# Starting nine convolution accumulators on TensorE, and feeding the low weight halves from SBUF

## The reference, cut to what matters

```python
def conformer_conv_mixer(h, w_in, conv_w, conv_b, ln_g, ln_b, w_out):   # h: 512 x 1024
    proj = h @ w_in                                                     # 512 x 6144
    val, glu_gate, z = jnp.split(proj, 3, axis=-1)                      # 2048 channels each
    u = val * jax.nn.sigmoid(glu_gate)
    u = causal_depthwise_conv(u, conv_w) + conv_b                       # 31 taps per channel
    u = jax.nn.silu(layer_norm(u, ln_g, ln_b))
    return (u * jax.nn.silu(z)) @ w_out
```

## Time and profile before

| what | value |
|---|---|
| median of 3 runs | 2544.98 us (2544.66 to 2545.96) |
| the profiled execution, its own time | 2544.66 us |
| its span | 2542.9 us |
| TensorE busy | 2498.4 us (98%) |
| VectorE, ScalarE, GpSimd busy | 1459.5, 1289.4, 1519.5 us |
| mean granted TensorE clock | 0.997 of full speed |
| layer A, first time | about 22 to 304 us of the span |
| layer A, second time | about 1401 to 1682 us of the span |

### The profile page before, as it was taken

The page is one execution under the profiler, slowest core; times in us unless marked ns, Lnnn a source line. Parts: engine busy times, 40 slices in busy tenths (PEclk is TensorE's granted clock), DMA queues, the critical chain, the costliest instruction groups (busy, mean ns, idle before and its releaser), DMA issues.

```text
span 2542.9 us, 31601 instructions
## 1 busy us (share of the span) xinstructions
PE 2498.4 (98%) x11897; PEld 2029.2 (80%) x11897; DVE 1459.5 (57%) x2426; ACT 1289.4 (51%) x1994; POOL 1519.5 (60%) x1018
## 2 busy tenths in 40 slices
PE   8999999999999999999999999999999999999998
PEld 6888787878888787888888888878877678788887
DVE  6999863064565614444441899976598752523202
ACT  6889644266566533222232888854245553423322
POOL 5999665443453555444465799957435547545653
PEclk9999999999999999999999999999999999999999
DMA  7888622255556222222222778842322232222221
GB/s 209 191 183 183 149 102 99 102 145 147 133 145 147 93 99 84 99 100 97 91 97 98 180 178 186 183 118 95 123 104 67 88 127 97 100 98 88 96 99 67
DMA packets 72019, 310.75 MB, mean 122 GB/s; under 512 B 8043, under 2 KB 8267, under 8 KB 58300
## 3 DMA queue, kind: packets, MB, share of 16 engines
q1 hardware_dynamic: 49308, 225.11, 26.2%
q0 software_dynamic: 22560, 83.62, 16.8%
HBM read 302.81 MB, written 5.89 MB: 121 GB/s over the span
## 4 chain that ended last, share of the span: by engine, by line
PE 80%; DVE 10%; POOL 4%; issue 3%; ACT 3%; DMA 1%; DVEq 0%; SPq 0%; POOLq 0%; ACTq 0%
PE ps L64 78%; DVE ps L81 3%; POOL AR L73 3%; DVE AR L81 2%; PE ps L67 2%; DVE AR L73 1%; DVE HL L81 1%; ACT AR L70 1%; DMA WL<-in_weights 1%; POOL WL L115 1%; DVE X L73 1%; ACT L70 0%; DMA AR<-in_x 0%; ACT WL L70 0%; ACT HH L70 0%
## 5 line engine op out<-in xcount | busy, mean ns | idle before, releaser
L64 PE MATMUL ps<-HH,WH 128*128 128x512 f32 x3080 | 1213.2, 394 | 4.3 <-ACT HH L70 1.2
L64 PE MATMUL ps<-HL,WH 128*128 128x512 f32 x3080 | 1192.2, 390 | 1.3 <-DVE HL L81 1.3
L64 PE MATMUL ps<-HH,WL 128*128 128x512 f32 x3080 | 1095.9, 390 | 5.5 <-DMA WL<-in_weights 5.5
L73 POOL TENSOR_TENSOR WL<-WR,WH 128x1024 fp32r<-128x1024 f32 x278 | 694.5, 2521 | 648.0 <-ACT WH L70 647.9
L64 PEld LDWEIGHTS ps<-HH,WH 128*128 128x128 f32 x3080 | 578.5, 188 | 142.0 <-issue 9.7
L64 PEld LDWEIGHTS ps<-HH,WL 128*128 128x128 f32 x3080 | 579.0, 188 | 127.9 <-DMA WL<-in_weights 6.5
L64 PEld LDWEIGHTS ps<-HL,WH 128*128 128x128 f32 x3080 | 578.8, 188 | 120.6 <-DVE HL L81 2.6
L70 ACT ACTIVATE WH<-WR 128x1024 fp32r<-128x1024 f32 (+1 forms) x405 | 410.3, 1046 | 444.4 <-PE ps L64 444.3
L81 DVE SCALAR_TENSOR_TENSOR ps<-AR,VEC,ps 128x512 f32<-128x512 f32 x648 | 446.3, 751 | 7.1 <-ACT ps L70 1.6
L73 POOL TENSOR_TENSOR AR<-AR 128x512 f32<-128x512 f32 x210 | 323.3, 1807 | 10.7 <-DVE AR L73 1.9
L115 POOL DMA_DIRECT2D WL<-in_weights x127 | 149.5, 1177 | 178.5 <-ACT WL L70 178.5
(11 more groups left out here) (180 smaller groups left out, 2084.0 us busy)
## 6 DMA issues: line engine op xcount, KB each, us to landing
WR<-in_weights SPq DMA_DIRECT2D x106, 1024.0 KB, 4.8
WR<-in_weights SPq DMA_DIRECT2D x194, 512.0 KB, 4.8
WL<-in_weights POOLq DMA_DIRECT2D x127, 512.0 KB, 7.6
AR<-negc_rows POOLq DMA_DIRECT2D x16, 640.0 KB, 4.3
gate_rows<-WR SPq DMA_DIRECT2D x14, 256.0 KB, 2.0
AR<-gate_rows SPq DMA_DIRECT2D x14, 256.0 KB, 3.7
AR<-in_x SPq DMA_DIRECT2D x2, 1024.0 KB, 6.0
AR<-bias_by_distance POOLq DMA_DIRECT2D x1, 2048.0 KB, 8.5
```

What stands on the lines that cost most here:

```text
L64: return Op(None if self.e is None else self.e.matmul(o, l, r, start=first, stop=last, skip_group_check=True))
L73: return Op(None if self.e is None else self.e.tensor_tensor(o, a, b, op))
```

## The change

- Each of the last nine of the twelve chains is begun by TensorE, not by ScalarE. TensorE multiplies by two diagonal fp32 matrices (the taps 30 and 29 of the tile's channels), so that such a chain has 29 taps left for VectorE and not 30. ScalarE makes the diagonals out of the identity matrix, in a ring of five tiles in HT.
- POOL_TAPS and the allowances change: GpSimd now does four whole tiles and 24 taps of one more, from slot 3 on.
- The accumulating DMA reads the raw weights from the raw slot in SBUF, not from HBM; a raw slot is loaded again only after that DMA has landed.
- The second halves of the z chunks (eight in each layer A) are no longer made with a DMA: GpSimd subtracts.
- In slots 0 and 1 ScalarE and GpSimd do their splits in another order relative to begins and products.

```diff
-            return i == 0 and n == 1 or i in HEAD_CHUNK[1:] or any(f < i < f + KE + KE // 2 or i == f + KE + KE // 2 + 1 for f in FIRST_A)
+            return i == 0 and n == 1 or i in HEAD_CHUNK[1:] or any(f < i < f + KE + (KE // 2 if n == 0 else 0) or i == f + KE + KE // 2 + 1 for f in FIRST_A)
...
-                    if summed(before[-1], n):
-                        sp.wait_ge(w_hi, before[-1], n, "low")
-                    else:
-                        sp.wait_ge(w_lo, before[-1], n)
+                    wait_low(sp, before[-1], n)
...
-                            l = l.rearrange("p k c -> p (k c)")
-                        pool.dma_add(l, weights[i][:, n * 1024:(n + 1) * 1024]).then_inc(w_sum[i % 2][n], i, by=16)
+                            l, r = (t.rearrange("p k c -> p (k c)") for t in (l, r))
+                        pool.dma_add(l, r).then_inc(w_sum[i % 2][n], i, by=16)
...
+        DIAG = [HT[:, i * P:(i + 1) * P] for i in range(5)]
...
-        POOL_TAPS = {0: 8, 1: 10, 3: PAD, 7: PAD, 8: PAD, 12: PAD, 15: 18}
+        POOL_TAPS = {2: PAD, 4: PAD, 7: PAD, 10: PAD, 12: 24}
         CHAIN = [i for i in range(KE) if POOL_TAPS.get(i, 0) < PAD]
+        PE_BEGINS = CHAIN[3:]
+        LAST_TAP = {i: PAD - 2 if i in PE_BEGINS else PAD - 1 for i in CHAIN}
+        BY_PE = [(i, k) for i in PE_BEGINS for k in (PAD, PAD - 1)]
...
-                room = PAD * KE if rest else 14 + slot % 2 if slot < KE else 7 + (slot % 3 == 0)
+                room = PAD * KE if rest else (15) if slot < KE else (7)
...
-                room = PAD * KE if rest else 8 - (slot % 4 == 3) if slot < KE else 4 - (slot % 4 == 3)
+                room = PAD * KE if rest else (8) if slot < KE else (3 + slot % 2)
...
+                for i in PLAN[slot]["begin"]:
+                    if i in PE_BEGINS:
+                        pe.wait_ge(a_u, j, i)
+                        wait_chain_bank(pe, j, i)
+                        for k in (PAD, PAD - 1):
+                            pe.wait_ge(a_diag, j, i, k)
+                            pe.mm(chain_bank(i)[:, :], DIAG[BY_PE.index((i, k)) % 5], U[i][:, k:k + T], k == PAD,
+                                  k < PAD).then_inc(a_init_p, j, i, k)
...
+        def diagonals_scalar(act, j, i):
+            for k in (PAD, PAD - 1):
+                n = BY_PE.index((i, k))
+                if n >= 5:
+                    act.wait_ge(a_init_p, j, *BY_PE[n - 5])
+                act.act(DIAG[n % 5], ident[:, :], ACT.Copy, scale=conv_w(j, k, i)).then_inc(a_diag, j, i, k)
...
         def begins_scalar(act, j, at):
             for i in at["begin"]:
-                act.wait_ge(a_u, j, i)
-                wait_chain_bank(act, j, i)
-                act.act(chain_bank(i)[:, :], U[i][:, PAD:], ACT.Copy, scale=conv_w(j, PAD, i)).then_inc(a_init, j, i)
+                n = CHAIN.index(i)
+                if i not in PE_BEGINS:
+                    act.wait_ge(a_u, j, i)
+                    wait_chain_bank(act, j, i)
+                    act.act(chain_bank(i)[:, :], U[i][:, PAD:], ACT.Copy, scale=conv_w(j, PAD, i)).then_inc(a_init_a, j, i)
+                if n + 1 < len(CHAIN) and CHAIN[n + 1] in PE_BEGINS:
+                    diagonals_scalar(act, j, CHAIN[n + 1])
...
                 if slot < KE:
-                    if slot != 1:
-                        split_hi(act, c0 + slot + 1, (0, 1) if slot == 0 else (1,))
+                    split_hi(act, c0 + slot + 1, (0, 1) if slot == 0 else (1,))
...
-                    if slot == 0:
-                        begins_scalar(act, j, PLAN[slot])
                     split_hi(act, c0 + slot + 2, (0,))
-                    if slot > 1:
-                        begins_scalar(act, j, PLAN[slot])
+                    begins_scalar(act, j, PLAN[slot])
                     products_scalar(act, j, n[len(n) // 2:])
```

More of the change, by code:

```diff
@@ L828, in build_program @@
         a_sig, a_u, a_zs = sig("a_sig"), sig("a_u"), sig("a_zs")
-        a_init, a_tap, a_ev = (sig(n) for n in ("a_init", "a_tap", "a_ev"))
+        a_diag, a_init_p, a_init_a, a_tap, a_ev = (sig(n) for n in ("a_diag", "a_init_p", "a_init_a", "a_tap", "a_ev"))
         a_prod, a_add, a_turn, a_mom = sig("a_prod"), sig("a_add"), sig("a_turn"), sig("a_mom")
@@ L841, in build_program @@
         REST = DGS[1]
+        DIAG = [HT[:, i * P:(i + 1) * P] for i in range(5)]
         MV, MRS = ST[:, 384:392], ST[:, 392:396]
         BY = MV.rearrange("p (b s) -> p s b", s=2)
-        POOL_TAPS = {0: 8, 1: 10, 3: PAD, 7: PAD, 8: PAD, 12: PAD, 15: 18}
+        POOL_TAPS = {2: PAD, 4: PAD, 7: PAD, 10: PAD, 12: 24}
         CHAIN = [i for i in range(KE) if POOL_TAPS.get(i, 0) < PAD]
+        PE_BEGINS = CHAIN[3:]
+        LAST_TAP = {i: PAD - 2 if i in PE_BEGINS else PAD - 1 for i in CHAIN}
+        BY_PE = [(i, k) for i in PE_BEGINS for k in (PAD, PAD - 1)]
         POOLED = sorted(POOL_TAPS)
-        SHARED = [i for i in POOLED if POOL_TAPS[i] < PAD]
         Z_LATE = 3
         def conv_plan():
-            taps = {i: list(range(POOL_TAPS.get(i, 0), PAD)) for i in CHAIN}
+            taps = {i: list(range(POOL_TAPS.get(i, 0), LAST_TAP[i] + 1)) for i in CHAIN}
             adds = {i: list(range(PAD)) if POOL_TAPS[i] == PAD else list(range(1, POOL_TAPS[i])) + [PAD] for i in POOLED}
@@ L1084, in layer_a_vector @@
                     else:
-                        dve.wait_ge(a_init, j, i)
+                        if i in PE_BEGINS:
+                            dve.wait_ge(a_init_p, j, i, PAD - 1)
+                        else:
+                            dve.wait_ge(a_init_a, j, i)
                         dve.wait_ge(a_u, j, i)
@@ L1130, in layer_a_vector @@
             scaled_vector(dve, 3 * j, 3 * j + 1, vec["norm_mix_2" if j else "b_norm"])
+        def diagonals_scalar(act, j, i):
[4 more added lines that the diff above has]
+                act.act(DIAG[n % 5], ident[:, :], ACT.Copy, scale=conv_w(j, k, i)).then_inc(a_diag, j, i, k)
         def evacuate_scalar(act, j, i):
-            act.wait_ge(a_tap, j, i, PAD - 1)
-            if i in SHARED and i != SHARED[0]:
-                wait_conv(act, j, SHARED[SHARED.index(i) - 1])
-            o = REST if i in SHARED else U[i][:, PAD:]
+            act.wait_ge(a_tap, j, i, LAST_TAP[i])
+            o = REST if i in POOL_TAPS else U[i][:, PAD:]
             act.act(o, chain_bank(i)[:, :], ACT.Identity, bias=a_vec("a_conv_b", j, i)).then_inc(a_ev, j, i)
@@ L1182, in layer_a_scalar @@
                 if slot < KE:
-                    if slot != 1:
-                        split_hi(act, c0 + slot + 1, (0, 1) if slot == 0 else (1,))
+                    split_hi(act, c0 + slot + 1, (0, 1) if slot == 0 else (1,))
                     starts_scalar(act, j, PLAN[slot])
                     products_scalar(act, j, n[:len(n) // 2])
-                    if slot == 1:
-                        split_hi(act, c0 + slot + 1, (1,))
                     act.wait_ge(a_gate, j, slot)
@@ L1277, in layer_a_gpsimd @@
                 if slot < KE:
-                    if slot != 1:
-                        split_lo(pool, c0 + slot + 1, (0, 1) if slot == 0 else (1,))
+                    split_lo(pool, c0 + slot + 1, (0, 1) if slot == 0 else (1,))
                     if j == 0 and slot == 0:
@@ L1282, in layer_a_gpsimd @@
                     conv_gpsimd(pool, j, n[:len(n) // 2])
-                    if slot == 1:
-                        split_lo(pool, c0 + slot + 1, (1,))
                     split_lo(pool, c0 + slot + 2, (0,))
```

## The result

| | before | after |
|---|---|---|
| median | 2544.94 us (2544.66 to 2545.96) | 2570.27 us (2569.61 to 2573.34) |
| the profiled execution, its own time | 2544.66 us | 2571.78 us |
| its span | 2542.9 us | 2570.0 us |

The medians are those of four executions each. The changed kernel is slower by 25.3 us: the ratio is 1.010, 95% interval 1.0087 to 1.0112. 2571.0 was predicted.

What follows compares the result with a forecast made beforehand. TensorE, full in the slots, was taken as the bound. First layer +16.4 - 5 - 0.5 = +10.9, second +16.4 - 1.4 - 0.3 + 0.3 = +15.0, together +26 on 2544.66: 2571 us, range 2557 to 2586.

Steps and rivals of the forecast that it cites:

- main term: Layers A: 36 added fp32 matmuls on TensorE, nothing hiding them, cost 16.4 us a layer, 32.8 us in all.
- The price of a product: TensorE's begins: one fp32 matmul on 512 columns takes 0.91 us, four times a rounded one; bounds 0.455 and 0.99.
- The rival of half price: TensorE's begins: a diagonal product costs only its two records, 0.455 us each, giving 2554 us; chance 0.10.
- The start: TensorE's wait at 28 us and the clock fall go, about 6 us, of which 5 are kept; bounds 0 and 6.5.
- the reload: Raw slots in layers A, loaded only after the sum lands: just hidden with a 7.6 us landing, in layer B nothing.
- the late refill: Layers A: sums from SBUF take 12 us, ScalarE stands 3 us in each of 16 slots; 2590 to 2600; chance 0.12.
- The first tap and the single chains: First layer A: VectorE's first tap at 37 to 39 us, single chains 0.79 us a tap, slot 7's U at 122 to 125.
- The tails and the stall: Layers A: stall at 1618.69 goes, -1.4 us; GpSimd waits around last turns, net -0.5 us first, -0.3 second layer.
- Its lower end: Low end of the range, 2557 us: main sum with 0.82 us a matmul, full start gain and both tails free.
- What was costed at nothing: Layers A: ScalarE's changed work is worth nothing on the path; VectorE's taps stay inside TensorE's two-slot lead and cost nothing.
- GpSimd's part: Layers A: twelve adds fewer give -15 us, eight subtractions for DMA issues +11; GpSimd ends a few us less late.
- the price of VectorE without cover: VectorE's single chains in layer A: if the cover were gone, some 1 us a slot for four slots.

Runs made afterwards that it cites:

- the third product: Changed kernel with a third diagonal product before each TensorE begin, overwritten by the next, against the changed kernel: 2584.7 us, 1.0153 to before.
- the plan's row in the table: New plan and z subtraction only, all begins on ScalarE, sums from HBM, early reload, against the kernel before: 2561.0 us, 1.0058.
- one product a chain: Changed kernel without the tap 29 product in each TensorE begin, 18 of 36 left out, against the changed kernel: 2564.3 us, 1.0076 to before.
- all sums from SBUF alone: Kernel before with all 127 sums read from SBUF and raw slots reloaded only after their sum, against the kernel before: 2553.1 us, 1.0024.

## Why the prediction was right

**The time and its main term.** 2571.0 was predicted, 2570.3 measured. That TensorE is the bound, has no idle time to hide the products and pays for all 36 of them is shown three ways: by the chain (1.70 us a pair), by TensorE's begins alone, which make the kernel before as slow as the whole change does, and by the third product, which costs its full 0.86 us in the second layer.

**The price of a product** was mis-sized a little: 0.91 was taken, 0.85 measured. So the term is 18 x 0.85 = 15.3 us a layer and not 16.4, 2.2 us less in both. The distance in the earlier trace rows had the lead-in of the first matmul in it, as the text there says. A product is 3.7 times the 0.228 us of an ordinary matmul. The Trainium skill ("FP8 and Floating Point Precision", TensorE Precision Notes) gives true fp32 four passes; the measured 3.7 bears this out better than it does two. The two records of 592 ns of a product in the profile do not show it; the distance between its neighbours does. The rival of half price has fallen with it.

**The start** gave at its own place what was forecast: the first sum landed after 5.42 us, at 27.7, TensorE had no wait and its clock stayed at 1.00. At the first turn it was 90.92 - 85.50 = 5.4 us ahead of before. The forecast kept 5 us for good; 5.4 - 3.26 - 1.7 = 0.4 were left behind the wait at 93 us. The step that failed is the reload. It was forecast just hidden, ScalarE without a wait over 1 us. In the timeline of ScalarE in the changed kernel stand (the last line is in the second layer):

```profile
36.83 1.06 ACT L70 ACTIVATE WH<-WR 128x1024 fp32r<-128x1024 f32 x1 [9.18 <-DMA WR<-in_weights]
...
69.98 1.06 ACT L70 ACTIVATE WH<-WR 128x1024 fp32r<-128x1024 f32 x1 [3.64 <-DMA WR<-in_weights]
...
128.91 1.06 ACT L70 ACTIVATE WH<-WR 128x1024 fp32r<-128x1024 f32 x1 [3.35 <-DMA WR<-in_weights]
...
161.89 1.06 ACT L70 ACTIVATE WH<-WR 128x1024 fp32r<-128x1024 f32 x1 [2.04 <-DMA WR<-in_weights]
...
1442.39 1.06 ACT L70 ACTIVATE WH<-WR 128x1024 fp32r<-128x1024 f32 x1 [7.41 <-DMA WR<-in_weights]
```

The sum of 7 us was about right in the median (5.4), but the one that TensorE waits for at 93 us took 8.18, and the loads took 8.61 and 10.10 us on the chain, against 4.6 in the median, while sums ran beside them. Such long loads are not new. In the kernel before, the DMA view at 26.5 us has

```profile
WR<-in_weights SPq DMA_DIRECT2D x1, 512.0 KB, 12.0
```

and ScalarE does not wait for it, because it was issued early. What is new is that the load is issued only when the sum has landed. The chain of the changed kernel also shows that the loads are not alone on this way: between the one of 8.61 us and the one of 10.10 lie VectorE's first 15 taps (39.45 to 50.5 us, one chain), the U behind them, and ScalarE, which waits 8.19 us for that U with the begin of chain 1 and splits the next chunks only then.

So the mechanism of the late refill was real, and it did not end with the first slots: ScalarE waits for raw loads, over 1 us, five times in the first layer and seven times in the second. But it reached TensorE only once, at 93 us, and was worth 5 us in all and not 20 to 25; later the slots that are longer by the products cover it. With the begins on ScalarE, in the same plan and with the same feeds, TensorE waits for sums six times in this layer. It took away what the start had given. That the two belong together is shown by the changed kernel with sums from HBM, which has neither and ends in the same time.

**The first tap and the single chains** came nearly as forecast: VectorE's first tap in the changed kernel at 39.45 us (37 to 39 forecast), 0.79 us a tap in a single chain, U of slot 7 at 123.14 (122 to 125 forecast). The U of slot 0 was begun at 30.26, so VectorE stood 8.50 us for a begin that ScalarE had queued behind its split, and the split behind the load:

```profile
39.45 11.84 DVE L81 SCALAR_TENSOR_TENSOR ps<-AR,VEC,ps 128x512 f32<-128x512 f32 x15 [8.50 <-ACT ps L70]
...
123.14 0.68 DVE L73 TENSOR_TENSOR AR<-ps,AR 128x512 f32<-128x512 f32 x1
```

**The tails and the stall** gave more than forecast. In the second layer the 1.44 us at 1618.69 went, as said, and about 1.1 us more around the last turns: 15.3 - 1.44 - 1.1 = 12.8, measured 12.7, forecast 15.0. In the first layer the 1.02 us in the earlier trace rows went, and the wait of 0.88 us in the earlier trace rows became 0.57: 15.3 - 0.4 - 1.3 = 13.6, measured 13.6, forecast 10.9.

**Sum.** 13.6 + 12.7 = 26.3 us for the layers, where 25.9 were forecast, and 0.8 more outside them: +2.4 that go with the clock and -1.6 that go with the z subtraction, which the forecast did not have. The main term and the bound are shown. That the total is right to 1 us is in part luck, because errors cancel: of the start's gain 4.6 us too much were kept, while the products (2.2 us) and the tails (about 2 us) were taken too dear. So the first layer became longer than forecast and the second shorter.

**Sums in the forecast that don't come out.** The idle time that it lists adds up to 12.1 us and not 13. Its lower end, put together as it says (0.82 us a product, 6.5 us at the start, both tails and the stall), is 2562 and not 2557, and a late refill that costs 20 to 25 us and the start's 5 is 2596 to 2601 and not 2590 to 2600. The main sum depends on none of the three.

**What was costed at nothing** is the weakest step, though the total doesn't show it. The plan, VectorE's taps and GpSimd's subtractions were "worth nothing on the path", and in the changed kernel they are. But the reason that the runs point to is that TensorE is 15 us a layer longer. Without this cover the plan with the z subtraction costs 15 us, the z subtraction on the old plan 22, the feeds 6 to 7. GpSimd's part was also mis-sized: a subtraction for a DMA issue takes 14 us a layer and not 11, so that with twelve adds fewer GpSimd is about level and not 4 us better off. The prediction gave 1 us a slot for four slots as the price of VectorE without cover, some 8 us for both layers; the plan's row in the table says 15, with the z subtraction in it, and which of the two has how much of this wasn't measured apart.

**Not settled.** Why a load beside sums takes twice as long wasn't tried by itself. Nor was the new order of ScalarE's and GpSimd's splits in slots 0 and 1: it stands in all kernels with the new plan and in none with the old one, and it is what puts the split of chunk 2 ahead of the begin of chain 0. With the begin first, VectorE might have started several us sooner. The clock differences outside the layers have no cause here.

## What to carry to other kernels

Where several engines are level within a few per cent (in the slots here TensorE 112.00, VectorE 110.49 and GpSimd 110.20 of 112.00 us), the costs of the parts of a change don't add: here they were 26, 15 and 6 us alone and 25 together, and taking the products, 26 us alone, out of the changed kernel gave 3. Run each part alone on the kernel before as well as taken out of the kernel after, before one of them is blamed or called free. And when a wait for a transfer is removed by making another transfer wait for it, look for the loss a few stages later, at the first place where the second one has no lead.

## What was unexpected of the hardware

- An fp32 product on 512 columns shows as two records of 592 ns, and takes 0.85 us of TensorE's stream.
- A 512 KB accumulating DMA reading SBUF lands in 5.4 us in the median, one reading HBM in 7.6; but single ones beside loads took 8.18, and loads beside them 8.61 and 10.10 us against 4.6. In the kernel before, with sums from HBM, loads beside them took 10.3 and 12.0 us. As fewer loads run beside a sum from SBUF here, the source alone may not be the reason for its 5.4 us.
- GpSimd goes on 0.60 us after it starts to issue a DMA whose span the profile gives as 1.10 us, and 2.37 us after the start of a 128x1024 subtraction whose span it gives as 3.51.
- After TensorE's wait of 3.26 us its clock was still 1.00 for the first microsecond of work, then 0.59 and 0.55 from 94 to 98 us. So that wait cost 1.7 us more than its own length, and the one at 28 us before the change 2.4 us more than its 4.09. The length of the last wait alone doesn't tell: after one of 2.89 us (one product a chain, at 92.46) the clock was 1.00 to 100 us, and after one of 1.94 (all sums from SBUF alone, at 150.15) it was 0.64 and 0.51 from 150 to 154.
